# Products of a zero block that nobody reads, on TensorE before and behind the first turning of a token tile

## The reference

```
h    = rms_norm(x) ; proj = h @ w_in
A    = gated delta rule over 4 heads (short conv + SiLU on q, k, v of proj; z gates the result)
B    = sliding-window attention over 8 heads (rotary on a quarter of the head, sinks)
x    = x + rms_norm(concat(A, B) @ w_out)
u    = conv3(rms_norm(x) @ w_up) ; y = (gelu(gate) * value) @ w_down
out  = x + rms_norm(y)
```

## Time and profile before

| what | value |
|---|---|
| median of 3 executions | 1221.24 us (1220.97 to 1221.99) |
| the profiled execution's own time | 1222.27 us |
| its span, first to last instruction | 1220.2 us |
| time around the span | 2.07 us |
| TensorE busy in the span | 1168.4 us, 96% |
| VectorE busy | 803.5 us, 66% |
| ScalarE, GpSimd busy | 44%, 32% |

### The profile page before, as it was taken

How to read it: one execution, slowest core, us unless ns; L and a number is a source line. 1 busy time by engine, 2 the same in 40 slices (tenths; PEclk the granted TensorE clock), 3 DMA queues, 4 the chain that set the end, 5 groups by cost and what they waited for, 6 DMA issues and landing times.

```text
span 1220.2 us, 16966 instructions
## 1 busy us (share of the span) xinstructions
PE 1168.4 (96%) x5964; PEld 987.4 (81%) x5964; DVE 803.5 (66%) x1135; ACT 540.3 (44%) x973; POOL 395.1 (32%) x353
## 2 busy tenths in 40 slices
PE   6999999998899999988699999999999999999997
PEld 5888888887888888876488888888888878888886
DVE  6333345467866677758678787787877867664457
ACT  5221143556355444435455444444444434653451
POOL 1222000211133332223346765557655561000001
PEclk9999999999999999999799999999999999999999
DMA  7322224446232223231144535445355557997613
GB/s 267 127 78 86 68 86 121 143 140 227 82 115 88 92 71 116 64 104 55 69 138 138 188 131 199 168 143 191 130 196 172 173 179 254 363 374 235 191 60 138
DMA packets 118292, 181.85 MB, mean 149 GB/s; under 512 B 20527, under 2 KB 78671, under 8 KB 113999
## 3 DMA queue, kind: packets, MB, share of 16 engines
q1 hardware_dynamic: 118223, 180.94, 44.1%
HBM read 123.21 MB, written 57.70 MB: 148 GB/s over the span
## 4 chain that ended last, share of the span: by engine, by line
PE 48%; DVE 3%; issue 1%; ACT 1%; POOL 0%; DVEq 0%; POOLq 0%; ACTq 0%
PE sums L2912 6%; PE sums L2913 6%; PE sums L2914 6%; PE f_ps_up L2912 6%; PE f_ps_up L2913 5%; PE f_ps_up L2914 5%; PE f_ps_up L2985 3%; PE f_ps_up L2986 3%; PE f_ps_up L2984 3%; PE sums L2986 2%; PE sums L2985 2%; PE sums L2984 2%; DVE h_t L2798 0%; ACT stage L2606 0%; DVE f_rest_raw L2695 0%
## 5 line engine op out<-in xcount | busy, mean ns | idle before, releaser
L2866 POOL TENSOR_TENSOR f_w_raw<-stage 128x512 f32<-128x512 f32 x44 | 69.4, 1578 | 136.5 <-PE f_ps_up L2914 132.8
L2620 DVE TENSOR_TENSOR f_w<-f_w_raw,f_w 128x512 fp32r<-128x512 f32 (+1 forms) x55 | 71.0, 1310 | 23.6 <-POOL f_w_raw L2866 23.5
L2870 POOL TENSOR_TENSOR conv<-conv 128x512 f32<-128x512 f32 x44 | 73.0, 1658 | 16.9 <-DMA conv<-in_w_down 14.3
L222 PE MATMUL sums<-split,slab_w 128*128 128x512 f32 x192 | 75.9, 395 | 0.5 <-PEq L273 0.5
L2870 POOL TENSOR_TENSOR f_conv<-f_conv 128x512 f32<-128x512 f32 x44 | 65.4, 1486 | 32.0 <-DMA y_blocks<-f_conv 28.6
L224 PE MATMUL sums<-split,slab_w 128*128 128x512 f32 x192 | 74.9, 390 | 0.0
L223 PE MATMUL sums<-split,slab_w 128*128 128x512 f32 x192 | 74.7, 389 | 0.0
L2912 PE MATMUL f_ps_up<-split,f_w 128*128 128x512 f32 x176 | 69.5, 395 | 4.4 <-DVEq L2616 3.7
L243 DVE SCALAR_TENSOR_TENSOR conv<-sums,conv_taps,conv 128x1023 f32<-128x1023 f32 (+6 forms) x39 | 46.8, 1199 | 37.3 <-ACT conv L234 36.4
L2913 PE MATMUL f_ps_up<-split,f_w 128*128 128x512 f32 x176 | 69.2, 393 | 0.0
L2914 PE MATMUL f_ps_up<-split,f_w 128*128 128x512 f32 x176 | 69.1, 393 | 0.0
(11 more groups left out here) (410 smaller groups left out, 3462.9 us busy)
## 6 DMA issues: line engine op xcount, KB each, us to landing
stage<-in_w_up SPq DMA_DIRECT2D x22, 1024.0 KB, 6.0
y_blocks<-f_conv SPq DMA_DIRECT2D x22, 1024.0 KB, 4.9
conv<-in_w_down SPq DMA_DIRECT2D x11, 1024.0 KB, 7.3
w_down_sums<-conv SPq DMA_DIRECT2D x11, 1024.0 KB, 10.5
stage<-y_blocks SPq DMA_DIRECT2D x40, 256.0 KB, 5.8
f_rest_raw<-y_blocks SPq DMA_DIRECT2D x37, 256.0 KB, 5.9
x_tile<-in_x SPq DMA_DIRECT2D x12, 512.0 KB, 4.3
stage<-in_w_in SPq DMA_DIRECT2D x6, 1024.0 KB, 6.7
```

The source lines that it names most:

```text
L222: pe.matmul(bank, w_hi, h_hi[:, k, cols], start=(k == 0), stop=False)
L2620: dve.tensor_tensor(out, src, hi.bitcast(F32), ALU.subtract).then_inc(s_lo[name], 1)
L2866: pool.tensor_tensor(raw_sum(m), a, b, op).then_inc(s_add[m], 1)
L2870: pool.tensor_tensor(view(out), view(a), view(b), op).then_inc(signal, 1)
```

## The change

VectorE's first act becomes the filling of the first 256 columns of `row` with zeros, and that instruction gives `s_mid` the count that a bare increment gave before. TensorE's stream opens with a wait for it and 18 products of the zeros with themselves (128 by 128, float32) into the first 128 columns of `ps_own`; only then comes the wait for the identity matrix. Seven more such products stand between the turning of tile 0 and the first products of tile 0. Nobody reads what they write, and the next writer of that bank starts its sum afresh.

```
@@ vector @@
-            for q in (s_z, s_mid, s_last):
+            dve.memset(row[:, 0:2 * P], 0.0).then_inc(s_mid, 1)
+            for q in (s_z, s_last):
                 dve.sem_inc(q, 1)
@@ tensor @@
+            def unread(count):
+                for _ in range(count):
+                    pe.matmul(ps_own[:, 0, 0:P], row[:, 0:P], row[:, P:2 * P], start=True, stop=True)
+
+            pe.wait_ge(s_mid, 1)
+            unread(18)
             pe.wait_ge(s_const, 16)
...
             front(0, 0)
+            unread(7)
             tiles(pe, tile)
```

## The result

The changed kernel takes 1224.9 us (median of 14 executions, 1222.15 to 1226.97), the kernel before 1221.37 us in as many beside it. The medians are 3.5 us apart and the means 2.9; the ratio is 1.0023 (95% interval 1.0014 to 1.0033): slower. I had forecast no change, 1221.2 us, and a range up to 1222.9. The profiled execution took 1224.89 us, the median, with a span of 1222.8; that of the kernel before lay 0.9 us above its median, so the two profiles differ by 2.6 us.

The account below looks back on a forecast made before the run. The prediction took VectorE's chain to bound tile 0, with TensorE 1.27 us to spare before its unbroken stretch from 27.14 us. Its terms summed 0 + 0 + 0 + 0 + 0: 1221.2 us, range 1219.9 to 1222.9.

Parts of the forecast that it names:

- The fill: VectorE's zeros at the program's start: 0.25 us, standing at about 1.0 us, no cost on the path.
- The 18 products: TensorE's zero products before the turning: 0.213 us each, 3.8 us, done at about 5.1, no cost.
- the upper bound of 7.7: The 18 products priced at 0.427 us each, the low pace of 512 columns; forecast as done at 8.9.
- my doubt whether the clock would fall again: TensorE's expected 3.2 us rest before the turning at 8.29 might lower the clock; rival of unraised or fallen clock, chance 0.25.
- The turning and the 7 products: Before tile 0: at the high clock the turning ends 0.9 us sooner and the 7 take 0.8 us, free.
- Tile 0 under VectorE: VectorE's chunks rule TensorE: group 2 starts at 27.14 again, the pause before it grows to about 2.1 us, no gain.
- So the time at which that stretch starts sets everything behind it, and the question is only whether 27.14 moves: TensorE's stretch without pauses from 27.14 to 180 us: its start decides all later times.
- The general shift: Added instructions may move code loading of later parts: either sign, up to 2.5 us or a little more, chance 0.04.
- The rival of the falling clock: The longer pause before group 2 at 27.14 lowers the clock: 1.7 us lost, 1222.9 us, chance 0.08.
- Less than 0.2%, 2.4 us, is about what a measurement of this kernel cannot tell from none: Threshold for the whole kernel's time: smaller differences count as no change, given chance 0.93.

Follow-up runs that it names:

- e7_padded: The whole change plus five already-reached waits behind the first product of each k in `multiply`, 228 instructions over the kernel before; ratio 0.9994 to the kernel before.
- e11_pad224_waits: The changed kernel without products, with 72 instructions of waits at TensorE's start and 152 in `multiply`; ratio 0.9992 to the kernel before.
- e5_waits72: The changed kernel with 124 waits for the 18 products and 20 for the 7, 72 instructions added, no product; ratio 1.0013 to the kernel before.
- e6_wide7: The changed kernel with 5 and 2 zero products of 512 columns for 18 and 7 of 128, 28 instructions added; ratio 1.0004 to the kernel before.
- e2_only18: The changed kernel without the 7 products behind the turning, the 18 kept, 72 instructions added; ratio 1.0018 to the kernel before.
- e8_again: The changed kernel once more, unchanged, 100 instructions added; ratio 1.0022 to the kernel before, profiled execution 1223.08 us.
- e1_fill_only: The changed kernel without all 25 products, the fill with zeros and its count kept; ratio 0.9999 to the kernel before.
- e3_only7: The changed kernel without the 18 products, the 7 behind the turning kept, 28 instructions added; ratio 1.0001 to the kernel before.

## Why the prediction was wrong, point by point

- *The fill*: 0.27 us at 0.87, against 0.25 taken. Right.
- *The 18 products*: mis-sized by a factor of two. The price of one MATMUL was right, 0.213 us at the low level and 0.111 at the high one, as the trace has them one by one. But a float32 product is two of them, and the earlier trace rows counts instructions and not products. The 36 took 7.1 us where I had 3.8; that this is inside the upper bound of 7.7 is luck (and with that bound they are done at 1.0 + 7.7 = 8.7, not at 8.9 as I wrote). The clock rose at 7.1 us while they ran. They reached to the turning without a rest, and my doubt whether the clock would fall again had no object.
- *The turning and the 7 products*: the turning right, 1.04 us. The 7 products took 1.73 us and not 0.8, by the same factor of two, but they were over at 10.7, before the 11.20 at which real products can start: their cost on the path is none, as forecast.
- *Tile 0 under VectorE*: right. Group 2 starts at 26.96 behind VectorE's 26.90, no low pace follows, and the stretch to 180 us is whole. The pause before it is 1.26 us and not 2.1: VectorE's first of four chunks in group 1 took 2.06 us and not a quarter of 5.47, and let TensorE start only at 19.95, where I had put 19.4. `e7_padded` and `e11_pad224_waits` show that the gain is indeed none.
- *"So the time at which that stretch starts sets everything behind it, and the question is only whether 27.14 moves"*: the step that failed. That start stayed where it was but for the 0.18 us of an earlier landing, and the end came 2.6 us later in the profile. A program's instructions are also data that is loaded, over the same DMA engines; adding 100 moved a fetch from 246.2 to 238.7 us, onto a transfer that VectorE waits for.
- *The general shift*, for which I gave 0.04 and "no row prices that": it was this, and the size was right. I counted 50 instructions, not 100, and did not look where the fetches of before stand, though the page counts them (q8 and q14) and the DMA view shows each. Its price could have been bounded from the fetch's own length, in the kernel before 0.9 to 1.6 us of one engine, times the transfers on the path that it might meet, plus a fall of the clock of at most half of 3.4 us.
- *The rival of the falling clock* named 1.7 us, 1.56 were measured, but in another place: the clock fell behind the pause at 248, not behind the one at 27. That the sizes agree is luck, since the low stretch at 323 from which I took the price leaves no mark on VectorE's chain.
- *"Less than 0.2%, 2.4 us, is about what a measurement of this kernel cannot tell from none"*: too wide. With 14 executions on each side the interval is 0.1% to either side, and it told 0.23% from none.

Settled by the runs: code without products (`e5_waits72`) loses, products with the fetch elsewhere (`e6_wide7`, `e7_padded`) do not. That the late share was on the very engine that carried the fetch follows from the packets, though they do not name engines. In `e2_only18` the fetch runs from 239.14 to 240.07 us; from 239.66 on no packet of the store is in flight, the next one starts at 240.05, and then 20 packets, 9.7 KB, run one behind the other until 240.87. `e5_waits72` and `e8_again` show the same (nothing of the store in flight for the last 0.44 and 0.22 us of the fetch, then 14.9 and 16.4 KB in a row); in the changed kernel it is less clean, with the rest of the share from 239.68 to 240.81. Open: whether the clock falls behind the longer pause (three of four profiles), and the scatter. `e5_waits72` ran from 1220.53 to 1227.31 us, three executions at or below 1221.2 and six above 1225, so the meeting or the fall may not be there in each; only profiled executions could tell.

## What to carry to other kernels

Before paying for a warmer clock, look at who releases the first long stretch of TensorE: here VectorE did, and up to 3 us of faster products became pauses. And treat added instructions as transfers: find the code fetches of the kernel before in the DMA view, estimate how far the new ones move, and check which short transfer with a waiting reader lies there. A small loss of 0.1 to 0.3% far behind an edit is a reason to compare one landing after another, and to repeat the edit with as many instructions that do nothing.

## What the runs showed of the hardware that I had not expected

- A code fetch of 16 KB takes 0.9 to 2.3 us on one of 16 DMA engines (all fetches of the fourteen profiles) and lengthened a 256 KB store from 3.1 to 3.4 us (ten profiles) to 4.5 to 4.8 (four). The Trainium skill ("DMA: Bandwidth & Descriptors", section "Queues, rings and completion order") lets an engine take turns between its queues at whole packets; `e2_only18` agrees: the store's packets on that engine go on 0.01 us before its fetch ends, and not sooner.
- SyncE's issue of a transfer also takes longer while a fetch runs: before, with one at 32.5 us,

```profile
32.45 1.64 SPq L396 DMA_DIRECT2D x_tile<-in_x  x1
```

and after, without one there,

```profile
32.26 0.43 SPq L396 DMA_DIRECT2D x_tile<-in_x  x1
```

- Products of zeros raise the clock: in the changed kernel nothing else ran on TensorE before the turning, their interval fell from 0.213 to 0.111 us at 7.1 us, and the turning took 1.04 us, against 1.94 in `e1_fill_only`. In `e3_only7` seven of them behind the turning bring tile 0 to the high pace at 13.75 us, against 15.80.
